# The second block's bias: reversed rows through TensorE, or repeated vectors read back from DRAM with a short row step

## What is computed

```
dist = qi + BLOCK - kj                          # qi 0..127, kj 0..255, BLOCK 128
band_ok = (dist >= 0) & (dist < WINDOW)         # WINDOW 128
bias = rel_bias[t5_causal_bucket(dist)]         # 32 buckets, 8 heads
logits = where(mask, logits + bias, NEG_INF)
```

## Time and profile before

| | us |
|---|---|
| median of 3 runs (2298.21 to 2300.68) | 2298.46 |
| the profiled execution | 2298.76 |
| its span, first to last instruction | 2296.9 |
| TensorE busy in it | 2267.5 |
| GpSimd busy | 881.3 |
| VectorE busy | 1254.7 |
| ScalarE busy | 837.2 |

### The profile page before, as it was taken

One profiled execution on the slowest core, in us unless ns is written; L12 is line 12 of the kernel. 1 busy time (PEld: TensorE's weight loads), 2 busy tenths in 40 slices (PEclk: granted clock), 3 DMA queues, 4 the chain that ended last, 5 costly groups with the idle time before them and its releaser, 6 DMA issues.

```text
span 2296.9 us, 29423 instructions
## 1 busy us (share of the span) xinstructions
PE 2267.5 (99%) x11709; PEld 1850.9 (81%) x11709; DVE 1254.7 (55%) x1575; ACT 837.2 (36%) x1024; POOL 881.3 (38%) x200
## 2 busy tenths in 40 slices
PE   9999999999999999999999999999999999999998
PEld 7888777888888888887778888887887777888887
DVE  5895445644447646954456543478466554620533
ACT  6334345332222333333344322222336644322322
POOL 2441333444444443423334444444433332444443
PEclk9999999999999999999999999999999999999999
DMA  6332333444445544323244444454963333443542
GB/s 160 85 74 56 74 71 77 92 97 103 92 91 134 142 101 92 74 56 70 60 91 92 92 97 102 94 135 111 167 161 74 74 74 74 92 101 84 108 101 74
DMA packets 193150, 218.13 MB, mean 95 GB/s; under 512 B 14608, under 2 KB 165272, under 8 KB 192408
## 3 DMA queue, kind: packets, MB, share of 16 engines
q1 hardware_dynamic: 192856, 216.63, 43.2%
q10 hardware_dynamic: 192, 0.05, 0.0%
HBM read 206.92 MB, written 9.73 MB: 94 GB/s over the span
## 4 chain that ended last, share of the span: by engine, by line
PE 50%; issue 34%; POOL 9%; DVE 3%; SPq 1%; DMA 1%; ACT 1%; DVEq 1%; POOLq 0%; ACTq 0%
PE psG L365 16%; PE psG L367 15%; PE psG L366 15%; POOL w_lo L2882 9%; PE psH L668 1%; DMA raw<-in_w_in_dram 1%; SPq L2055 1%; PE psH L2247 0%; ACT w_hi L358 0%; DVE tab L1792 0%; PE psH L693 0%; PE psH L2211 0%; DVE s L1792 0%; DVE x2t L2851 0%; DVEq L1906 0%
## 5 line engine op out<-in xcount | busy, mean ns | idle before, releaser
L2882 POOL TENSOR_TENSOR w_lo<-raw,w_hi 128x2048 fp32r<-128x2048 f32 x184 | 874.5, 4753 | 1396.3 <-ACT w_hi L358 1336.9
L365 PE MATMUL psG<-h_hi,w_hi 128*128 128x512 f32 x1640 | 647.4, 395 | 1.9 <-POOL w_lo L2882 1.3
L358 ACT CAST w_hi<-raw 128x2048 fp32r<-128x2048 f32 x184 | 351.3, 1909 | 815.8 <-PE psG L367 794.8
L366 PE MATMUL psG<-h_lo,w_hi 128*128 128x512 f32 x1640 | 638.8, 390 | 0.0
L367 PE MATMUL psG<-h_hi,w_lo 128*128 128x512 f32 x1640 | 638.6, 389 | 0.0
L365 PEld LDWEIGHTS psG<-h_hi,w_hi 128*128 128x128 f32 x1640 | 307.8, 188 | 82.1 <-issue 18.3
L367 PEld LDWEIGHTS psG<-h_hi,w_lo 128*128 128x128 f32 x1640 | 307.9, 188 | 65.1
L366 PEld LDWEIGHTS psG<-h_lo,w_hi 128*128 128x128 f32 x1640 | 308.0, 188 | 63.6 <-issue 1.4
L2819 DVE TENSOR_TENSOR hq<-r 128x512 f32<-128x512 f32 x32 | 81.0, 2569 | 146.2 <-ACT r L2585 146.0
L365 PE MATMUL psG<-hid_hi,w_hi 128*128 128x512 f32 x352 | 138.5, 394 | 2.0 <-POOL w_lo L2882 2.0
L367 PE MATMUL psG<-hid_hi,w_lo 128*128 128x512 f32 x352 | 137.7, 391 | 0.0
(11 more groups left out here) (506 smaller groups left out, 3227.6 us busy)
## 6 DMA issues: line engine op xcount, KB each, us to landing
raw<-in_w_in_dram SPq DMA_DIRECT2D x121, 512.0 KB, 6.3
raw<-in_w_gate_dram SPq DMA_DIRECT2D x44, 512.0 KB, 6.4
raw<-in_w_up_dram SPq DMA_DIRECT2D x44, 512.0 KB, 5.9
raw<-in_w_down_dram SPq DMA_DIRECT2D x32, 512.0 KB, 6.5
raw<-in_w_ff_in_dram SPq DMA_DIRECT2D x32, 512.0 KB, 6.2
raw<-in_w_ff_out_dram SPq DMA_DIRECT2D x32, 512.0 KB, 6.0
raw<-in_w_o_dram SPq DMA_DIRECT2D x16, 512.0 KB, 6.0
raw<-in_w_down_dram SPq DMA_DIRECT2D x16, 384.0 KB, 5.2
```

The costliest lines, as they stand in the source:

```text
L358: act.copy(w_hi[:, s, :], raw[:, s, :]).then_inc(hi_done.sem, 1)
L365: pe.matmul(out, a_hi, b_hi, start=first, stop=False)
L366: pe.matmul(out, a_hi, b_lo, start=False, stop=False)
L2882: pool.tensor_tensor(w_lo[:, s, :], raw[:, s, :], w_hi[:, s, :].bitcast(F32), ALU.subtract)\
```

## The change

The bias rows are no longer turned on TensorE. SyncE stores each head's vector 128 times, one copy behind the other, so that DRAM holds 8 x 128 rows of 384 numbers; it does so in four DMAs of two heads each, behind the loads of units 3, 4, 5 and 6. The read in the second block steps by 383 numbers from row to row, and so finds each row moved by one place. It is four DMAs with rows of 1 KB in place of two with rows of 2 KB. Gone are `exch`, the read `t5_up`, the four matmuls, ScalarE's four copies and the store `bias_d`, with the waits that belonged to them. `t5_rows` moves to an address that no later table uses.

```
-    t5_dram = nc.dram_tensor("t5_dram", (QH, 3 * P), F32, kind="Internal").ap()
+    t5_dram = nc.dram_tensor("t5_dram", (QH, P, 3 * P), F32, kind="Internal").ap()
...
-    t5_rows = hat("t5_rows", 8.5, [QH, 3 * P])
+    t5_rows = hat("t5_rows", 30.5, [QH, 3 * P])
...
-        if l == 0 and u == 3:
-            sp.wait_ge(made_dve.sem, T5_OK)
-            sp.dma_start(t5_dram, t5_rows[:, :]).then_inc(st_t5.sem, 16)
-            sp.wait_ge(st_t5.sem, 16)
-            with nc.allow_non_contiguous_dma(reason="overlapping rows"):
-                sp.dma_start(t5_up[:, :, :], bass.AP(t5_dram.tensor, 0, [[1, P], [3 * P, QH], [1, 2 * P]]))\
-                  .then_inc(ld_t5.sem, 16)
-        if l == 0 and u == 6:
-            sp.wait_ge(made_act.sem, BIAS_OK)
-            sp.dma_start(bias_d, bias_s[:, :, :].rearrange("p h k -> p (h k)")).then_inc(st_bias.sem, 16)
+        if l == 0 and 3 <= u < 7:
+            if u == 3:
+                sp.wait_ge(made_dve.sem, T5_OK)
+            two = slice(2 * u - 6, 2 * u - 4)
+            sp.dma_start(t5_dram[two], t5_rows[two, :].unsqueeze(1).broadcast_to([2, P, 3 * P])).then_inc(st_t5.sem, 16)
...
-            act.wait_ge(st_bias.sem, 16)
+            act.wait_ge(st_t5.sem, 64)
...
             pe.wait_ge(ld_c.sem, 64)
-            pe.wait_ge(made_act.sem, BIAS_OK)
...
-        if l == 0 and u == 2:
-            pe.wait_ge(consts.sem, 8)
-            pe.wait_ge(ld_t5.sem, 16)
-            pe.wait_ge(made_dve.sem, ROW_OK)
-            for n in range(4):
-                mm = pe.matmul(psH[:, n, :], exch[:, :], t5_up[:, 2 * n:2 * n + 2, :].rearrange("p a b -> p (a b)"),
-                               start=True, stop=True)
...
-        if l == 0 and u == 2:
-            act.wait_ge(made_pe.sem, FLIP_MM)
-            for n in range(4):
-                act.copy(bias_s[:, 2 * n:2 * n + 2, :].rearrange("p a b -> p (a b)"), psH[:, n, :])
-            act.drain().then_inc(made_act.sem, 1)
...
         dve.drain().then_inc(made_dve.sem, 1)
-        dve.wait_ge(st_bias.sem, 16)
...
-        sp.wait_ge(st_bias.sem, 16)
+        sp.wait_ge(st_t5.sem, 64)
         for h in range(2):
-            sp.dma_start(bias[:, 4 * h:4 * h + 4, :].rearrange("p (g j) k -> p g (j k)", g=2),
-                         bias_d.rearrange("p (g h jk) -> p h g jk", g=2, h=2)[:, h]).then_inc(ld_bias.sem, 16)
+            for g in range(2):
+                sp.dma_start(bias[:, 4 * h + 2 * g:4 * h + 2 * g + 2, :],
+                             bass.AP(t5_dram.tensor, (4 * g + 2 * h) * P * 3 * P + P - 1,
+                                     [[3 * P - 1, P], [P * 3 * P, 2], [1, 2 * P]])).then_inc(ld_bias.sem, 16)
```

More of the change, by code:

```diff
@@ L146, in build_in @@
     stat = sb("stat", [P, 2, 8])
-    exch = sb("exch", [P, P])
     d_col = sb("d_col", [P, CT])
@@ L1582, in build_in @@
     TW = 2 * PAIRS * (CT + 1 + CT + 2 * GC)
-    bias_d = nc.dram_tensor("bias_d", (P, QH * 2 * P), F32, kind="Internal").ap()
     tab_d = nc.dram_tensor("tab_d", (P, TW), F32, kind="Internal").ap()
@@ L1605, in build_in @@
     s_log = hat("s_log", 7.875, [16, 2, NS])
-    t5_rows = hat("t5_rows", 8.5, [QH, 3 * P])
+    t5_rows = hat("t5_rows", 30.5, [QH, 3 * P])
     c_tok = hat("c_tok", 10, [P, 2, 4, 2, NS])
     b_re, b_im = hat("b_re", 14, [P, PAIRS, GC]), hat("b_im", 15, [P, PAIRS, GC])
-    t5_up = hat("t5_up", 16, [P, QH, 2 * P])
-    bias_s = hat("bias_s", 24, [P, QH, 2 * P])
     HP = PAIRS // 2
@@ L1620, in build_in @@
     rot_tmp = hat("rot_tmp", 16.5, [P, 2, PAIRS, CH // 2])
[L1622 to L1626, removed]
+    ld_t, ld_c, ld_b, ld_sink, ld_tab = sem("ld_t"), sem("ld_c"), sem("ld_b"), sem("ld_sink"), sem("ld_tab")
+    st_t5, st_tab, st_win, st_wt, st_kern, st_rot = (sem("st_t5"), sem("st_tab"), sem("st_win"), sem("st_wt"),
+                                                     sem("st_kern"), sem("st_rot"))
     made_dve, made_pe, made_act = sem("made_dve"), sem("made_pe"), sem("made_act")
     LOG_OK, T5_OK, ROW_OK, ANG_OK, TAB_OK, E_OK, WT_OK, K_OK, ROT_OK = 1, 2, 3, 4, 5, 6, 8, 10, 11
-    ROW_TR, FLIP_MM, C_TR, WIN_TR, K_MM = 1, 2, 3, 4, 6
-    DT_OK, MAG_OK, BIAS_OK, WIN_OK = 1, 2, 3, 4
+    ROW_TR, C_TR, WIN_TR, K_MM = 1, 2, 3, 5
+    DT_OK, MAG_OK, WIN_OK = 1, 2, 3
     def tables_sync(sp, l, u):
@@ L1722, in tables_pe @@
                                       c_tok[:, r, t, :, :].rearrange("p a b -> p (a b)"), ident[:, :])
-            mm.then_inc(made_pe.sem, 1)
-        if l == 0 and u == 2:
-            pe.wait_ge(consts.sem, 8)
-            pe.wait_ge(ld_t5.sem, 16)
-            pe.wait_ge(made_dve.sem, ROW_OK)
-            for n in range(4):
-                mm = pe.matmul(psH[:, n, :], exch[:, :], t5_up[:, 2 * n:2 * n + 2, :].rearrange("p a b -> p (a b)"),
-                               start=True, stop=True)
             mm.then_inc(made_pe.sem, 1)
@@ L1737, in tables_pe @@
             else:
-                pe.wait_ge(made_act.sem, BIAS_OK)
+                pe.wait_ge(made_act.sem, MAG_OK)
             for i in range(2 * HP):
@@ L2105, in second_sync @@
         sp.wait_ge(st_out.sem, 32 * TB)
[L2107 to L2111, removed]
     r_h2 = rms
@@ L2707, in second_dve @@
         gate_scaled(dve, 5)
-        dve.wait_ge(ld_bias.sem, 32)
+        dve.wait_ge(ld_bias.sem, 64)
         def gated(gate, u, k, v, pairs=(0, 1)):
@@ L2875, in _ @@
         setup_pool(pool)
-        second_pool(pool)
         def low_parts(first, end):
```

## The result

| | us |
|---|---|
| before, median of 5 runs beside it | 2298.46 |
| with the change, median of 5 runs (2309.47 to 2313.92) | 2311.84 |
| ratio, 95% interval | 1.0055 [1.0044, 1.0066] |
| profiled execution with the change | 2312.89 |
| its span | 2311.1 |

The change makes the kernel slower by 13.4 us; 2308.7 was predicted, in a range of 2297.4 to 2318.5.

A forecast was written before the change was run, and what follows sets the result against it. TensorE, busy 2267.5 of 2296.9 us, was taken as the bound. Late weights behind the four stores add 10.2 us, the freed 3.43 us lying inside this sum: 2298.46 + 10.2 = 2308.7 us, range 2297.4 to 2318.5.

The forecast's parts named there:

- Off TensorE, 3.43 us: First layer's down projection: without the four reversal matmuls, unit 3 starts at 722.39 in place of 725.82, freeing 3.43 us.
- That they don't last: Two units on, TensorE waits about 1.6 us before unit 5 and the rest at tables E; 0.3 us gain taken.
- 12.0 us per part: Each 384 KB store goes over two engines, one per source partition, 192 KB each at 62.5 ns per KB: 12.0 us.
- the break-even: Store length of 9.4 us per part, below which casts stay ahead of TensorE and the four stores cost nothing.
- the shared door: Rival: a part's two source partitions hinder each other behind one port; about 14.5 us per part, +20, 2318.7; chance 0.20.
- The queue sum, +10.2: From 710.9, four stores and the weights between them take 63.0 us; unit 7's `w_lo` ends at 781.6 against 771.42: +10.2 us.
- the term of the weights between them: Loads of units 4, 5 and 6 between the four stores on the two engines: 4.0, 3.0 and 4.0 us.
- the step from the last store to unit 7: After the last store: unit 7's weights 4.0 us, landing 1.1, cast 1.91, 0.1 between, `w_lo` 4.60.
- What would show it: Signs: stores 12 us or more apart, casts of units 5 to 7 waiting for DMA, TensorE waiting some 10 us net.
- The rest, at nothing: ScalarE's copies, GpSimd's `exch` work and dropped waits cost nothing; four bias reads near 1664 cost 0 to 0.3 us.

The follow-up runs named there:

- Both edits together: Version filling the rows by one DRAM-to-DRAM copy, plus ScalarE's squares behind the next cast and transposes of E one unit later: 2295.93 us against 2298.72 before.
- partitions four apart: The changed kernel with each of the four stores taking two vectors four partitions apart (heads 0 and 4, and so on): 2298.54 us against 2298.80 before.
- the version with the DRAM copy: The changed kernel without its four stores: 12 KB stored once, then copied 128 times inside DRAM by one DMA: 2299.85 us, ratio 1.0004 to before.
- ScalarE's queue: The changed kernel with its four stores issued by ScalarE behind the casts of units 3 to 6, not by SyncE: 2302.36 us, ratio 1.0012.
- squares later: The DRAM-to-DRAM copy version with ScalarE's squares of the first two pairs of the first layer moved behind the next unit's cast: 2305.02 us, ratio 1.0026.
- transposes later: The DRAM-to-DRAM copy version with the transposes of E behind units 6 and 7 in place of 5 and 6: 2298.26 us, ratio 0.9997.
- the matmuls put back there: The DRAM-to-DRAM copy version with four matmuls of the removed ones' size put back behind unit 2: 2298.12 us, ratio 0.9996.

## Why the prediction was right, and where its reason was not

**Off TensorE, 3.43 us.** Right. Both edits together, an execution that lies 0.28 us later than the one before, has the transposes of C at 733.33; 733.06 was predicted for an undelayed start:

```profile
733.33 1.03 PE L1712 MATMUL psH<-ident,c_tok 128*128 128x128 f32 x8
```

**That they don't last.** Right, to the place and the size. About 1.6 us of wait before unit 5 and the rest at E were forecast; with partitions four apart, where the stores do no harm, TensorE waits just there:

```profile
748.87 0.50 PE L364 MATMUL psG<-hid_hi,w_hi 128*128 128x512 f32 x1 [1.63 <-POOL w_lo L2851]
...
759.43 1.97 PE L1721 MATMUL psH<-ident,Et 128*128 128x128 f32 x16 [2.11 <-DVEq L1887]
```

Put back, the matmuls cost nothing. When both holds, ScalarE's squares ahead of unit 5's cast and the early transposes of E, were taken away at once, 2.8 us came through.

**12.0 us per part.** This step is wrong in its mechanism, and the time is near only because two errors go against each other. Two engines carry a part, as taken. But an engine whose partition shares its group of four with no other needs 65 ns for 1.5 KB, 43 ns per KB, not the 62.5 worked out from `out` and `rot_d`. That pair of rows compares landings, which hold more than an engine's own rate: the packets of these stores took 86 ns for 2 KB and 309 ns for 8 KB, 39 to 43 ns per KB. Alone, the two engines take 8.0 to 8.7 us, below the 9.4 of the break-even, and the forecast's own mechanism would have meant no change in time: the version with partitions four apart shows it. What makes a part 13.2 to 15.8 us, 14.1 in the mean, is the shared door, a rival with 0.20 and not the forecast. It was given 14.5 us per part (the middle of its 10 and 20 is 15) and 2318.7 us; the first is near, the second 6.9 us too long, from the sum below. That 2308.7 lies only 3.1 us from the measured time is luck.

**The queue sum, +10.2.** Right in form: it forecast the first store at 710.9, or 713.1 with this execution's late start, and its first packet starts at 713.22. From there 48 us of stores and 11 of weights between them were to end at 772.1; they end at 777.4. The stores took 56.4 (8.4 more), the gaps between them 7.8 (3.2 less). The cast of unit 7 starts at 781.70, its `w_lo` ends at 788.22, and TensorE starts at 788.27. So 14.65 us in place of 10.2: the term that was too small is the parts', by 2.1 us each, and the term of the weights between them gave back 3.2 us; the step from the last store to unit 7 was 0.8 shorter than forecast. The range held the time, since it reached to the shared door.

**What would show it.** The signs named came but for one: stores 12 us or more apart (the first two only 10.7), casts of units 5 to 7 waiting for the DMA, TensorE waiting for `w_lo`, 10.0 us in sum, with 1.93 of them before unit 4. The 2.8 us at E were not foreseen. The copy of E on ScalarE stands behind the late cast of unit 7, but that wait lies inside the delay, since unit 7 waits for its own `w_lo` right after it.

**The rest, at nothing.** Right. The four bias reads took 4.58 us of issue on SyncE, 0.65 more than the two, and the delay did not grow behind them.

**Left out of the sum: TensorE's clock.** The working has every matmul at 0.227 us. Here this made no difference to unit 7, which waited for its weights in any case; in the version with the DRAM copy it is 1.7 us.

## What to carry over

A DMA whose source has few partitions is costed twice: by the engines that carry it, and by the groups of four partitions that these read from; here another choice of two rows, and so of their places in DRAM, was worth 13 us. Whatever waits behind such a store in its queue pays for it. Filling the rows from DRAM cost nothing that could be measured; a queue with no weights took away 10 of the 13 us. And work taken off the bound engine only shows when all that arrives just in time, two and three steps on, is brought forward too: one hold removed alone gave nothing or made it worse, both gave 2.8 us.

## What the runs showed that was not expected

**Fast first, then slow.** Two engines in one group of four partitions ran at 65 ns per packet for 3 to 4 us in each part of the change, and at 118 to 125 ns from then on. In the version with ScalarE's queue, where each store begins as the one before ends, the first store's packets took 118 ns from the start, and those of the others changed between 65 and 123 without such an order. Why was not found out.

**TensorE's clock after waits.** Behind three of its waits, of 1.93, 4.35 and 2.92 us, TensorE's granted clock fell. Windows of the change; the figure ahead of the last two is the mean granted clock:

```profile
739.00:743.00 4.00, 4.00 (x12) 3.13 (x11) 3.66 (x7) 1.06 (x1) 0.00 (x0) 0.57 0.13 27
756.00:760.00 4.00, 4.00 (x12) 3.12 (x11) 3.85 (x4) 0.00 (x0) 0.00 (x0) 0.57 0.12 28
769.50:773.50 4.00, 3.43 (x9) 2.74 (x10) 0.97 (x1) 0.00 (x0) 0.42 (x1) 0.57 0.54 138
```

In part of each window the clock is at 1.2 in place of 2.4 GHz, with matmuls 0.43 us apart in place of 0.227; a mean of 0.57 over 4 us is a loss of 1.7 us of full clock. It did not set the change's time, because unit 7 waited for its weights anyway. But it makes waits dearer where nothing absorbs it: with squares later, behind the wait of 8.0 us, the clock was 0.75 from 762 to 770 us. With partitions four apart, waits of 1.6 and 2.1 us left it at 1.00.

The length of the wait does not decide it. One wait of 2.03 to 2.05 us for `w_lo`, between 1582 and 1604 us, stands in all twelve traces; behind it the clock fell in five of them (before, transposes later, both edits with the DRAM copy, the matmuls put back there, ScalarE's queue) and stayed in seven. The execution of before, and that of the change:

```profile
1587.00:1591.00 4.00, 4.00 (x12) 3.09 (x12) 0.73 (x1) 2.13 (x4) 4.00 (x1) 0.57 0.74 167
...
1603.00:1607.00 4.00, 3.44 (x15) 2.85 (x16) 1.59 (x1) 2.98 (x5) 3.92 (x2) 1.00 0.48 109
```

Each kernel has one trace, so that two executions of one kernel differ in this is not seen there; but the mean granted clock of the 21 runs of the kernel before beside the first experiments lies between 0.996 and 0.999. The 1.7 us of one such stretch are more than several of the differences above.
